# Thirty of thirty-one chunk transposes moved from TensorE and PSUM to VectorE and SBUF, in blocks of 32 partitions

## The reference

```
x = x + sliding_window_attention(rms_norm(x), ...)
x = x + (silu(h @ w_gate) * (h @ w_up)) @ w_down          # 11 chunks of 512 hidden features
y = sigmoid(o) * rmsnorm(mlstm(q, k, v, gates)) * silu(z)  # 8 heads of 512 features
x = x + ... y @ w_out
k, v = kv_projection(...);  q, z = projection(...)
x = x + ... (band_attention(q, k, v) * silu(z)) @ w_out    # 4 groups of 4 heads
```

## Time and profile before

| | |
|---|---|
| three runs | 2425.92, 2426.9 and 2427.5 us, median 2426.9 us |
| the profiled execution's own time | given as its span alone, 2424.4 us, 2.5 us below the median of the runs |
| PE busy | 2408.2 us, 99% of the span |
| DVE, ACT, POOL busy | 1726.8, 1170.0 and 45.2 us |
| granted TensorE clock | 0.999 of full speed |

### The profile page before, as it was taken

How to read it: one execution, slowest core, us unless ns; L and a number is a source line. 1 busy time by engine, 2 the same in 40 slices (tenths; PEclk the granted TensorE clock), 3 DMA queues, 4 the chain that set the end, 5 groups by cost and what they waited for, 6 DMA issues and landing times.

```text
span 2424.4 us, 31019 instructions
## 1 busy us (share of the span) xinstructions
PE 2408.2 (99%) x11417; PEld 1960.0 (81%) x11417; DVE 1726.8 (71%) x2422; ACT 1170.0 (48%) x1583; POOL 45.2 (2%) x65
## 2 busy tenths in 40 slices
PE   9999999999999999999999999999999999999998
PEld 7778888888888888778888888888888778888887
DVE  8885777777777776667778667677676676667665
ACT  6665444444444444554444434444444564455553
POOL 1100000000000000000000000000000000000000
PEclk9999999999999999999999999999999999999999
DMA  8445888888888887567777787767777467776654
GB/s 299 141 136 175 265 292 294 307 294 293 284 296 292 291 297 228 163 225 237 241 232 234 239 265 244 237 231 235 240 232 240 156 193 255 242 238 212 232 192 139
DMA packets 161829, 578.16 MB, mean 238 GB/s; under 512 B 18288, under 2 KB 20592, under 8 KB 161680
## 3 DMA queue, kind: packets, MB, share of 16 engines
q1 hardware_dynamic: 160432, 572.64, 71.3%
q0 software_dynamic: 1104, 3.28, 0.4%
q10 hardware_dynamic: 144, 0.26, 0.0%
HBM read 574.01 MB, written 2.10 MB: 238 GB/s over the span
## 4 chain that ended last, share of the span: by engine, by line
PE 96%; DVE 2%; ACT 1%; DMA 1%; issue 0%; POOL 0%; SPq 0%; DVEq 0%; ACTq 0%
PE PS L1177 30%; PE PS L1179 30%; PE PS L1178 30%; PE PS L796 1%; DVE WL L2165 1%; PE PS L908 1%; DMA X<-in_x 0%; ACT WH L1552 0%; PE PS L803 0%; PE PS L876 0%; DVE X L2132 0%; PE PS L1004 0%; PE PS L1078 0%; PE PS L1024 0%; PE PS L1021 0%
## 5 line engine op out<-in xcount | busy, mean ns | idle before, releaser
L2165 DVE TENSOR_TENSOR WL<-W,WH 128x1024 fp32r<-128x1024 f32 x814 | 991.2, 1224 | 528.6 <-ACT WH L1552 526.0
L1552 ACT ACTIVATE WH<-W 128x1024 fp32r<-128x1024 f32 x814 | 857.4, 1060 | 923.0 <-PE PS L1179 912.6
L1177 PE MATMUL PS<-WH,XTH 128*128 128x512 f32 x2144 | 855.3, 399 | 3.6 <-DVE XTL L1683 1.2
L1179 PE MATMUL PS<-WH,XTL 128*128 128x512 f32 x2144 | 835.9, 390 | 0.0
L1178 PE MATMUL PS<-WL,XTH 128*128 128x512 f32 x2144 | 835.0, 389 | 0.0
L1177 PEld LDWEIGHTS PS<-WH,XTH 128*128 128x128 f32 x2144 | 402.6, 188 | 94.5 <-issue 10.1
L1179 PEld LDWEIGHTS PS<-WH,XTL 128*128 128x128 f32 x2144 | 402.3, 188 | 85.7
L1178 PEld LDWEIGHTS PS<-WL,XTH 128*128 128x128 f32 x2144 | 402.9, 188 | 83.6 <-issue 3.8
L1177 PE MATMUL PS<-WH,YTH 128*128 128x512 f32 x1120 | 441.0, 394 | 2.5 <-DVE WL L2165 1.8
L1179 PE MATMUL PS<-WH,YTL 128*128 128x512 f32 x1120 | 436.2, 389 | 0.0
L1178 PE MATMUL PS<-WL,YTH 128*128 128x512 f32 x1120 | 436.1, 389 | 0.0
(11 more groups left out here) (282 smaller groups left out, 1171.3 us busy)
## 6 DMA issues: line engine op xcount, KB each, us to landing
W<-in_vec SPq DMA_DIRECT2D x192, 512.0 KB, 4.6
W<-in_avoz SPq DMA_DIRECT2D x192, 512.0 KB, 4.5
W<-in_wg SPq DMA_DIRECT2D x88, 512.0 KB, 4.7
W<-in_wu SPq DMA_DIRECT2D x88, 512.0 KB, 4.9
W<-in_wd SPq DMA_DIRECT2D x88, 512.0 KB, 4.7
W<-in_gate SPq DMA_DIRECT2D x64, 512.0 KB, 4.4
W<-in_aqk SPq DMA_DIRECT2D x64, 512.0 KB, 4.4
W<-in_aout SPq DMA_DIRECT2D x64, 512.0 KB, 4.3
```

The lines of the kernel that those rows point to most:

```text
L1177: e.matmul(p, x, WH[:, g % NH, j], start=first, stop=False)
L1179: i = e.matmul(p, y, WH[:, g % NH, j], start=False, stop=last)
L1552: e.activation(WH[:, n % NH], W[:, i % NW], ACT.Copy).then_inc(s_hi, 1)
L2165: e.tensor_tensor(l, src, h.bitcast(F32), ALU.subtract).then_inc(s_lo, 1)
```

## The change

30 of the 31 chunk transposes leave PE (11 of `ffn`, 8 of `mix`, 4 of `keys`, 4 of the queries, 3 of the 4 band outputs; the last band's stays). In their place DVE turns each chunk with 16 `transpose` instructions of 32 partitions: block row a of the source, all four blocks b of both tiles in one instruction (256 elements on each of 32 partitions), written to the partitions of block row b. They write a new SBUF tile `MT`, or `KT` and `Q4` directly. ACT and DVE then make `YTH` and `YTL` from `MT`. Two blocks go by per tick, four in `band`. `MT` costs 4 KB in each partition; POOL's DMA scratch is set to 8192 bytes.

```
+            def blocks_T(dst, src, n, sem):
+                for x in range(16):
+                    a, b = slice(32 * (x // 4), 32 * (x // 4) + 32), 32 * (x % 4)
+                    o = dst[b:b + 32].rearrange("p j (t r) -> p t j r", t=2)[:, :, :, a]
+                    i = e.transpose(o, src[a].rearrange("p t (j k) -> p t j k", j=4)[:, :, :, b:b + 32])
+                    if x == 15:
+                        i.then_inc(sem, 1)
+                    if x % n == n - 1:
+                        yield
+            def pair_lows(k0, scale):
+                for x in (0, 2):
+                    n_y[0] += 1
+                    w.wait_ge(s_yh, n_y[0])
...
+            def pairs_T(number, k0, scale):
+                w.wait_ge(s_mt, number)
+                for x in (0, 2):
+                    if scale is None:
+                        i = e.activation(YTH[:, k0 + x:k0 + x + 2], MT[:, x:x + 2], ACT.Copy)
...
 (PE, band)
-                yield from to_T("qT", 4 + j)
+                yield from ticks(6)
...
-                    w.wait_ge(s_kq, 8 + 2 * j + 2)
+                    w.wait_ge(s_kq, 4 + j + 1)
...
 (DVE, ffn)
-                yield from ticks(5)
-                for half in range(2):
-                    lows_Y(("mid", f, half), 4 * slot, None)
-                    yield
+                yield
+                w.wait_ge(s_mid, 2 * f + 2)
+                yield from blocks_T(MT, MID, 2, s_mt)
+                yield from ticks(2)
+                yield from pair_lows(4 * slot, None)
...
 (DVE, band, ahead of its scores)
-                yield from ticks(6)
+                yield
+                w.wait_ge(s_qc0, 4 + j + 1)
+                w.wait_ge(s_qc1, 4 + j + 1)
+                if j:
+                    w.wait_ge(*filled(("bs", 4 * j - 1)))
+                yield from blocks_T(Q4, QC, 4, s_kq)
+                yield
...
 (DVE, band, behind them)
+                if j < N_BY_DVE:
+                    yield
+                    w.wait_ge(s_bo, 4 * j + 4)
+                    yield from blocks_T(MT, ZG, 4, s_mt)
+                    yield from ticks(2)
+                    yield from pair_lows(4 * j, None)
+                    return
```

More of the change, by code:

```diff
@@ L1227, in halves_T @@
                 i.then_inc(s_yh, 1)
+            def pairs_T(number, k0, scale):
[3 more added lines that the diff above has]
+                        i = e.activation(YTH[:, k0 + x:k0 + x + 2], MT[:, x:x + 2], ACT.Copy)
+                    else:
+                        for j in (x, x + 1):
+                            i = e.activation(YTH[:, k0 + j], MT[:, j], ACT.Copy, scale=scale(k0 + j))
+                    i.then_inc(s_yh, 1)
+                    yield
             def turn_x(n, k, g):
@@ L1369, in ffn @@
                     e.activation(SGT[:, t], Gb[ends[0][0]][t][:, :], ACT.Silu, scale=rst[:, t:t + 1]).then_inc(s_sg, 1)
-                yield from ticks(21)
-                for half in range(2):
-                    w.wait_ge(s_unit, free)
-                    halves_T(("mid", f, half), 4 * slot, None)
-                    yield
+                yield from ticks(27)
+                w.wait_ge(s_unit, free)
+                yield from pairs_T(MT_FFN + f + 1, 4 * slot, None)
             def gate_w(g):
@@ L1435, in mix @@
                 e.activation(SG[:, 512:1024], Gb[ends[3][0]][1][:, :], ACT.Sigmoid).then_inc(s_mixa, 1)
[L1436 to L1455, removed]
+                yield from ticks(12)
+                base = CGH + 4 * h - 4 * (h % 4)
+                w.wait_ge(s_unit, free)
+                yield from pairs_T(MT_MIX + h + 1, 4 * (h % 4), lambda kt: cols[:, base + kt:base + kt + 1])
             def qc(n, par, g):
@@ L1510, in band @@
                 yield from band_order(score_, turn, pv, lambda: j in zdone)
+                if j < N_BY_DVE:
+                    yield from ticks(6)
+                    w.wait_ge(s_unit, free)
+                    yield from pairs_T(MT_BAND + j + 1, 4 * j, None)
+                    return
                 yield from ticks(4)
@@ L2017, in mix @@
                     yield
-                yield from ticks(5)
-                for half in range(2):
-                    base = CGH + 4 * h - 4 * (h % 4)
-                    lows_Y(("mixT", h, half), 4 * (h % 4), lambda kt: cols[:, base + kt:base + kt + 1])
-                    yield
+                w.wait_ge(s_mix, at("y1"))
+                yield from blocks_T(MT, G1, 2, s_mt)
+                yield from ticks(2)
+                base = CGH + 4 * h - 4 * (h % 4)
+                yield from pair_lows(4 * (h % 4), lambda kt: cols[:, base + kt:base + kt + 1])
             def qc(n, par, g):
@@ L2026, in qc @@
                 if n:
-                    w.wait_ge(*filled(("kT" if n <= 4 else "qT", n - 1, 0)))
-                    w.wait_ge(*filled(("kT" if n <= 4 else "qT", n - 1, 1)))
+                    w.wait_ge(s_kq, n)
                 e.tensor_copy(QC[:, 1], Gb[par][1][:, :]).then_inc(s_qc1, 1)
@@ L2033, in keys @@
                 yield
+                w.wait_ge(s_qc0, j + 1)
+                w.wait_ge(s_qc1, j + 1)
+                w.wait_ge(s_post, 8)
+                yield from blocks_T(KT[:, 4 * j:4 * j + 4], QC, 2, s_kq)
             def values(j, par, g):
```

62 lines of the change are left out of this document (27 added, 35 removed).

## The result

The changed kernel takes **2470.6 us** (median; 2468.4 to 2471.9), the kernel before 2426.6 beside it: ratio 1.0179, 95% interval 1.0165 to 1.0193, so 44 us slower. The prediction said 2452 us, range 2427 to 2475. The profiled execution of the changed kernel took 2468.43 us, its span is 2466.7.

What follows compares the result with a forecast made beforehand. PE was taken to bound the kernel, busy 99% of the span. Terms -25.5 + 37.8 + 3 + 4 + 1 + 5 = +25.3 on a span of 2424.4 gave 2449.7, forecast as 2452 us; range 2427 to 2475.

Steps and rivals of the forecast that it cites:

- the room left above for late `WL`: Upper part of the range 2427 to 2475, said to take in some mixture of late weights on DVE.
- What PE saves: PE's transposes: 0.85 us saved per chunk, 30 chunks, 25.5 us in all.
- The block: DVE's transposes: distance d from block to block taken as 0.45 us, between bounds of 0.32 and 0.68.
- The bands: First score of later bands waits for DVE's queue: 12.6 us each, 37.8 us for three.
- First band: First band's score, with no `ZG` blocks ahead, waits for DVE's query blocks: 3 us.
- The clock: Three idle stretches of PE of about 12 us may each bring back the slower clock: 3 x 1.7 = 5 us.
- The mixer: Eight heads: about 0.5 us lost per head, since ACT waits for the last block ahead of a `WH`; 4 us.
- It just holds: Mixer: DVE's queued `WL` would end at 1287.2 to 1300.4, against due times of 1289.3 to 1300.2.
- The keys: `KT` is needed only by the bands; the first falls together with `second`, and the same count gives 1 us.
- The feed-forward, "I count 0": Feed-forward, 11 chunks: blocks and `MID` eat 5.1 of 5.5 us of slack over four units, so 0 us lost.
- The slack of 5.5 us: Time DVE's `WL` has to spare: 8.16 us for three units, less about 2.6 for ACT's `WH` and DVE's `WL`.
- the rivals' terms: Overlapping blocks 2433 us, chance 0.15; faster than before, 0.12; within 0.2%, 0.10; half-rate transposes 2540 us, 0.08.

Runs made afterwards that it cites:

- warm_wait: Changed kernel, with 50 TensorE matmuls on ones ahead of its wait at the first score of bands two to four; 2463.81 us, ratio 1.0155.
- late_turn: Changed kernel, queries and band outputs turned by TensorE; in feed-forward (but its last chunk) and mixer, YTH and YTL two ticks later; 2426.71 us, ratio 1.0000.
- spread: Changed kernel, one block per tick, YTH later; TensorE also turns the four queries and the last feed-forward chunk; 2424.07 us, ratio 0.9990.
- selected: Changed kernel, one block per tick; TensorE turns fourth and last feed-forward chunks, first keys, all queries and band outputs; 2410.88 us, ratio 0.9937.
- selected_two: Same 20 chunks on VectorE as selected, but two blocks per tick as in the changed kernel; 2418.00 us, ratio 0.9969.
- same_quadrant: Changed kernel, each chunk's 16 blocks reordered so the output stays in the same 32 partitions for four in a row; 2471.21 us, ratio 1.0188.
- bands_alone: Changed kernel, but only the four queries and three band outputs on VectorE, the 23 other chunks on TensorE; 2468.64 us, ratio 1.0176.
- block_twice: Kernel of selected, with each block of the second keys turned twice in a row, into KT and then MT, two per tick; one run, 2413.97 us.

## Why the prediction held, and where its sum fell short

The direction and the place were right; the sum was 17 us short in the span (2449.7 against 2466.7). That the result lies in the range is owed to the room left above for late `WL`, which no row had priced.

- **What PE saves**, 0.85 us per chunk. Measured at each place as 0.87 (0.74 where the transposes stood and 0.13 at the next half). Right.
- **The block**, d = 0.45. Measured 7.18 us for 16 and 436 ns for one, 0.449 from start to start. Right, and with the reason given: no overlap while the output moves.
- **The bands**, 12.6 us for each of three. PE's waits there are 0.97 + 11.15 = 12.1, and warm_wait shows 12.4 to 12.8 with the clock kept up. First band 3: PE's wait is 3.39 us, its jump with the late matmuls behind it 5.1.
- **The clock**, 1.7 us three times. warm_wait gives 4.5 us for the three by the matched matmuls, 5.8 to 6.8 by the times, where I had 5. Right for these three, but it fell twice more, which the sum had at nothing: behind the first band's wait of 3.39 us (granted clock 0.72 from 2154 to 2160) it cost 1.7 us, behind the fourth feed-forward chunk 2.5. These stand in the 5.1 and the 6.4 us of their places.
- **The mixer**, 4 us: 6.1, about 0.76 per head where I had 0.5. The number was near by luck. "It just holds" is wrong by the prediction's own dates: with the 0.85 us of the old transposes taken off, the last `WL` (1300.4) is due at 1299.3 and comes 1.05 late; at this head 1.1 us were lost. And the reason given, ACT's wait ahead of a `WH`, isn't the one: behind this head, where PE waited, `WH` had ended over 7 us before PE started, and late_turn, which cut ACT's waits behind the heads from 25.1 to 4.5 us, changed nothing.
- **The keys**, 1 us: 4.0. I had taken the first keys as one more burst; the start of the third layer loads DVE at the same time. spread lost 3.3 there even at one block per tick, and selected, with the first keys on PE, lost nothing.
- **The feed-forward, "I count 0"**: this is the step that failed, 11.2 us. What DVE has to do was counted rightly: in the six chunks that start with a lead of 5.64 us the nearest `WL` still ended 0.6 to 1.5 us ahead of PE, near the 0.4 of the count (5.1 of 5.5 eaten). The slack of 5.5 us, set for all 11, is what doesn't hold. The first three chunks come behind a small unit of the gate vector and start with 3.4 to 5.0, and their items are 0.15 us longer: they lost 1.2, 0.6 and 0.9 us. The fourth comes behind one and falls on the late load as well: 6.4. The last lost 1.7 on its `YTL`, which the count left out. selected_two against selected shows the density at work (7 us, the mixer included), spread against selected the places.

The change did what it says; L796's successor keeps 16 matmuls. Of the signs that were named, the four waits at the score came, and so did the fall of the clock. PE's busy time fell by 10 us, not by 25; part of the rest are matmuls at the lower clock (0.63 us in place of 0.39 at 2222.19). The waits for `WL` were to stay below 10 us and came to 10.2, but 4.1 us more stand under another name at 443.32. In the rivals' terms, d settled all of those that needed less or more than 0.45.

What I first held against the result, that ACT's wait ahead of a `WH` makes the weights late, late_turn refuted. I had read the longest wait on ACT (78.6 us in 14 times at `YTH<-MT`) as a cause; it was as late as DVE's queue, and nothing more.

Open: how the 6.4 us of the fourth chunk divide between the late load and the blocks. Seven other runs have blocks at two per tick there (same_quadrant in another order): they gave back 4.5 to 8.4 us, and DVE's item behind the load began 1.7 to 4.4 us after the start of the last unit ahead of PE's wait (2.5 in the changed kernel). By and large more was lost where it began later. Where TensorE turned this chunk (bands_alone, selected), it began 1.1 us after, and 0.3 to 0.4 us were lost. Why the load comes when it does wasn't looked into. That the short lead is what the first three chunks lack was read from traces and not tried apart. The changed kernel's smaller DMA scratch has no run of its own; in bands_alone, which has it, the matmuls up to the bands stand within 0.9 us of the kernel before.

## What to carry to other kernels

Work moved off the bounding engine is free only if every place where it lands has slack for it, counted with what stands in that very stretch and with how far ahead the engine is when the stretch begins: one slack for all places hides the few that give everything back. Match the same instructions of two traces by number and subtract their starts; the jumps name the places, and leaving the change out there (here 11 of 31) turned a kernel 1.8% slower into one 0.3% faster, and with half the density 0.6%. Ahead of a product that waits at once for its operand, a slow path on another engine costs its whole queue, and a wait of 11 us costs 1.5 to 2 us more in clock. Waits of 3.4 to 5 us cost 1.7 to 2.5 more here where the clock fell.

## What the runs showed that was not expected

VectorE's transpose of 256 f32 elements on 32 partitions takes 0.436 us. Two in a row overlap by 0.07 us if both read and write the 32 partitions of the one before (0.37 from start to start); else the distance is 0.449 (0.41 between the pairs of block_twice, whose second block takes 0.40). The two merged rows of 256 elements in the earlier trace rows overlap by 0.09 (0.407 less 0.32), and the earlier trace rows have 409 to 481 ns, so a transpose is neither faster nor slower than the other operations of its size.
